# Gated embedding and down bias on four row strips, the loop's bias product on eight 32x32 tiles

## The chip, the cores and the metric

One Trainium2 chip, one of its cores, one launch. The metric is the device time of the whole program in microseconds (us). TensorE is PE here, VectorE DVE, ScalarE ACT, GpSimd POOL, and SP the engine that issues most transfers.

## The reference, cut to what matters

The program runs two blocks on 512 tokens of width 1024, in fp32: a block of four mixers with a mixture of experts and a gated embedding, and then a second block of two layers. The change touches the experts' biases and the gated embedding:

```python
hg, hl = jnp.split(xblk @ w_gu[e] + b_gu[e], 2, axis=-1)     # every block of rows, of one expert e
...
y = sum over the 4 chosen experts of gate * (hidden @ w_down[e] + b_down[e])
ffn = alpha * x1 + y
x = layer_norm(ffn + sigmoid(ffn @ ple_gate) * (p @ ple_proj), ln2)   # the gated embedding
x = layer_norm([meta, x], ln_emb)                                      # the second block begins
```

The lines of `y` and below are written here in short for what the reference does in several functions.

## The kernel before

The program is written engine by engine, and each engine runs its instructions in the order in which they are written; semaphores tie the engines together. Three stretches matter.

**The loop over row blocks.** 32 iterations, each for 96 routed rows of one expert. PE multiplies with the gate and up weights (line 1350, 96 matmuls of 512 columns, four at a time on four 32-column strips of the array), then fetches the expert's bias row (`bias_rows`, line 1338), and then multiplies with the down weights (line 1432, 96 matmuls of 256 columns). `bias_rows` multiplies a one-hot [32 x 32] with the table of biases `b_all`, which lies as four quarters on four strips of 32 partitions; quarter j goes to PSUM partitions 32j to 32j+31 of bank 6. ACT copies the bank to `b_gu` (line 2279). Once ahead of the loop the same product and copy run for the first block. A profile shows each fp32 matmul as two records, one for each of its two passes over the array. SP loads the expert's six pieces of 2 MB (line 1893) as PE frees their slots.

**down_bias.** Behind the loop PE turns the gates of the four tiles of 128 tokens (`transpose`, shown as line 908) into rows 0 to 31 of one bank, DVE copies them to `gates_t` (line 3045), and PE multiplies each tile's gates with `b_down` in eight matmuls of depth 32, tile by tile (line 1330). All use partitions 0 to 31. DVE adds each result to alpha times `x1` into `ffn` (line 3050). Then DVE adds the four chosen experts' rows of each tile (line 3121); they are read back from memory by SP in one 2 MB load for each tile (line 1929). The load of tile 3 is issued when tile 0 is added, since it takes its place.

**gated_embedding.** PE makes 8 embedding products (`embed`, line 1453; a tile's half of 512 columns each) in `v_ring`, a ring of PSUM banks 0 to 2 that DVE frees, and 8 gate products (line 1468) in `a_ring`, banks 3 to 5, which ACT frees. Three embeddings go ahead of the gates and the others between them, with a claim of their bank each. ACT turns each gate product into a sigmoid (line 2295) and after a tile's two halves computes the two square roots of that tile's norms (`rows_root`, line 2046), for each of which it waits for DVE. DVE multiplies sigmoid and embedding (line 3136), adds to `ffn` (line 3137) and norms the tile twice. The norm of the 16 meta rows, the second block's first rows, stands behind tile 0's rows of line 3121. `layers()` follows; PE enters it when both rings are empty.

Of the kernel before, what the change touches and what calls it, by code (L numbers as in the profile page):

```python
# [20 lines left out]
P = 128  # L21
# [8 lines left out]
E = 32  # L30
# [436 lines left out]
def build(nc, io):  # L467
    with ExitStack() as ctx:
# [146 lines left out]
        gates_t = take(SEQ)  # L615
# [37 lines left out]
        h_t = y_t  # L653
# [246 lines left out]
        def _(pe):  # L900
# [369 lines left out]
            def mix_out():  # L1270
# [25 lines left out]
                for half in range(2):  # L1296
                    w = ws[half]
                    for t in range(TT):
# [7 lines left out]
                        if half == 1 and t >= 2:  # L1306
                            if t == 2:
                                pe.wait_ge(sem("router_landed"), 16 * 4)
                                pe.wait_ge(v_ring.drained, len(MIX_BANKS))
                            router(t - 2, jobs[t - 2])  # L1310
# [9 lines left out]
            def down_bias():  # L1320
                pe.wait_ge(sem("gates_ready"), 1)
                bank = v_ring.bank(pe)
                for t in range(TT):
                    mm = transpose(bank[0:E, t * P:(t + 1) * P], gates[:, t, :])
                job = v_ring.ship(mm)
                pe.wait_ge(v_ring.drained, job)
                for t in range(TT):
                    for half in range(2):
                        bank = v_ring.bank(pe)
                        v_ring.ship(pe.matmul(bank, gates_t[0:E, t * P:(t + 1) * P], b_down[0:E, half * 512:(half + 1) * 512],  # L1330
                                              start=True, stop=True))
# [113 lines left out]
            def gated_embedding():  # L1445
# [3 lines left out]
                def embed(n):  # L1449
                    t, half = divmod(n, 2)  # L1450
                    bank = v_ring.bank(pe)
                    for k in range(2):
                        mm = pe.matmul(bank, p_t[:, k, t * P:(t + 1) * P], w_proj[:, k * D + half * 512:k * D + (half + 1) * 512],  # L1453
                                       start=(k == 0), stop=(k == 1))
                    v_ring.ship(mm)

                for n in range(3):
                    embed(n)
                w = []
                turned_job = transposed_tile(ffn, 0, sem("ffn_ready"))  # L1460
                for t in range(TT):
                    pe.wait_ge(a_ring.drained, turned_job)
                    for half in range(2):
# [6 lines left out]
                        if 3 <= 2 * t + half + 2 < 2 * TT:  # L1470
                            embed(2 * t + half + 2)
# [355 lines left out]
            pe.wait_ge(v_ring.drained, v_ring.sent)  # L1827
# [3 lines left out]
        def _(sp):  # L1831
# [46 lines left out]
            sp.dma_start(b_down[0:E, :], io["b_down"]).then_inc(sem("router_landed"), 16)  # L1878
# [132 lines left out]
        def _(act):  # L2011
# [248 lines left out]
            def experts():  # L2260
# [6 lines left out]
                A.did(act.copy(b_gu, psum[:, BIAS_BANK, :]), bias_ready)  # L2267
# [1443 lines left out]
```

## Time and profile before

| | us |
|---|---|
| median of 3 runs | 3166.81 (3165.43 to 3167.59) |
| the profiled execution, its time | 3164.56 |
| its span, first to last instruction | 3162.7 |
| PE busy in the span | 3049.8 (96%) |
| the loop's line 1350 / 1432 / 1338 on the chain that ended last | 21% / 11% / 1% of the span |
| mean granted TensorE clock | 0.975 of full speed |

The span is what the profile's rows divide; the time of an execution is 1.9 us more. A row "20.60 PE psum L1350 x192" of the chain says that 192 records of line 1350 followed one another for 20.60 us with nothing else on the chain between them.

### The profile page before, as it was taken

How to read it: one execution, taken by the hardware profiler on the slowest of the kernel's cores; microseconds unless marked ns; L12 is line 12 of the kernel's file. 1: busy time of each engine (PE TensorE's matmuls, PEld its weight loads, DVE VectorE, ACT ScalarE, POOL GpSimd, SP SyncE). 2: the span in 40 equal slices, each digit the busy share in tenths (PEclk: the TensorE clock that was granted, in tenths of full speed). 3: DMA queues.
4: the chain of work that ended last, by engine and by line, in shares of the span. 5: the costliest groups of instructions: out<-in, count | busy, mean ns of one | idle time of the engine just before them, and what ended most of it. 6: DMA issues, size and time to landing. Idle time of an engine off the chain costs nothing.

```text
span 3162.7 us, 53140 instructions
## 1 busy us (share of the span) xinstructions
PE 3049.8 (96%) x22625; PEld 1725.8 (55%) x22625; DVE 1218.2 (39%) x2417; ACT 559.4 (18%) x1138; POOL 225.7 (7%) x288
## 2 busy tenths in 40 slices
PE   9888979999999999999999999999999999999999
PEld 3355545434343434333345667674786658675865
DVE  1633365332322223232365452436325462435131
ACT  1332231111111111111122220140102310140000
POOL 0000000221212121212100000000000000000000
PEclk9988979999999999999989999999999999999999
DMA  4100115999999999999863333343424253343442
GB/s 165 40 15 27 35 39 213 365 410 405 415 407 403 413 406 411 405 412 408 333 268 117 134 111 126 126 151 149 167 111 169 108 209 125 119 167 124 189 168 90
DMA packets 68398, 684.44 MB, mean 216 GB/s; under 512 B 12092, under 2 KB 14396, under 8 KB 25408
## 3 DMA queue, kind: packets, MB, share of 16 engines
q1 hardware_dynamic: 53488, 651.87, 51.9%
q0 software_dynamic: 11296, 26.05, 2.2%
q10 hardware_dynamic: 3504, 4.94, 0.5%
q8 instruction: 83, 1.36, 0.2%
q14 instruction: 27, 0.22, 0.0%
HBM read 675.00 MB, written 16.80 MB: 219 GB/s over the span
## 4 chain that ended last, share of the span: by engine, by line
PE 84%; DVE 4%; ACT 2%; issue 1%; DMA 0%; DVEq 0%; SPq 0%; ACTq 0%
PE psum L1350 21%; PE psum L1743 20%; PE psum L1720 11%; PE psum L1432 11%; PE psum L1677 3%; PE psum L1666 3%; PE psum L908 1%; PE psum L1468 1%; PE psum L1302 1%; PE psum L926 1%; PE psum L1784 1%; PE psum L1338 1%; PE psum L1524 1%; PE psum L1570 1%; PE psum L1453 1%; PE psum L1598 1%
## 5 line engine op out<-in xcount | busy, mean ns | idle before, releaser
L1350 PE MATMUL psum<-weight_ring,arena 128*32 128x512 f32 x6192 | 670.4, 592 | 0.0
L1743 PE MATMUL psum<-arena,weight_ring 128*128 128x256 f32 (+1 forms) x2816 | 636.0, 384 | 2.8 <-ACT arena L2394 2.8
L1743 PEld LDWEIGHTS psum<-arena,weight_ring 128*128 128x128 f32 x2816 | 528.3, 189 | 100.3 <-issue 12.9
L1350 PEld LDWEIGHTS psum<-weight_ring,arena 128*32 128x32 f32 x6192 | 201.5, 110 | 449.1 <-issue 434.1
L1432 PE MATMUL psum<-weight_ring,arena 128*32 128x256 f32 x6144 | 338.2, 380 | 0.0
L1432 PEld LDWEIGHTS psum<-weight_ring,arena 128*32 128x32 f32 x6144 | 196.9, 110 | 152.7 <-issue 26.8
L1720 PE MATMUL psum<-weight_ring 128*128 128x512 f32 x468 | 204.1, 593 | 4.9 <-DMA weight_ring<-down 3.6
L1720 PE MATMUL psum<-weight_ring,arena 128*128 128x512 f32 x470 | 206.1, 597 | 0.7 <-ACT arena L2394 0.7
L3460 DVE TENSOR_TENSOR weight_ring<-weight_ring,psum 128x256 f32<-128x256 f32 (+1 forms) x88 | 37.4, 425 | 430.4 <-PE psum L1743 428.3
L3105 DVE STREAM_TRANSPOSE arena<-arena 128x384 f32<-128x384 f32 x32 | 18.5, 579 | 457.5 <-PE psum L1350 457.5
L3360 DVE TENSOR_TENSOR weight_ring<-weight_ring 128x1024 f32<-128x1024 f32 (+1 forms) x140 | 157.2, 1172 | 9.3 <-PE psum L1720 9.0
L1720 PEld LDWEIGHTS psum<-weight_ring 128*128 128x128 f32 x468 | 88.5, 190 | 116.0 <-issue 108.8
L1720 PEld LDWEIGHTS psum<-weight_ring,arena 128*128 128x128 f32 x470 | 89.5, 191 | 112.8 <-issue 111.1
L3081 DVE TENSOR_TENSOR arena<-psum,arena 128x512 f32<-128x512 f32 x96 | 65.1, 678 | 210.2 <-PE psum L1350 210.2
L924 PE MATMUL psum<-arena,weight_ring 128*128 128x512 f32 x288 | 133.6, 614 | 10.9 <-DMA weight_ring<-weights 6.6
L2454 ACT ACTIVATE weight_ring<-psum 128x256 f32<-128x256 f32 (+1 forms) x88 | 34.0, 387 | 584.0 <-PE psum L1743 583.8
L2277 ACT ACTIVATE arena<-arena 128x256 f32<-128x256 f32 x96 | 40.1, 417 | 468.8 <-DVE arena L3083 468.8
L1677 PE MATMUL psum<-arena,weight_ring 128*128 128x272 f32 (+1 forms) x512 | 116.8, 386 | 0.0
L1677 PEld LDWEIGHTS psum<-arena,weight_ring 128*128 128x128 f32 x512 | 96.1, 189 | 19.9 <-issue 2.8
L1965 POOL DMA_INDIRECT arena<-token_rows,arena x99 | 101.1, 1021 | 80.1 <-DVE arena L3073 31.9
L1989 POOL DMA_INDIRECT y_tokens<-arena x96 | 97.0, 1011 | 49.7 <-POOL arena L1985 28.3
L924 PEld LDWEIGHTS psum<-arena,weight_ring 128*128 128x128 f32 x288 | 54.2, 195 | 76.6 <-issue 67.0
(468 smaller groups left out, 2850.5 us busy)
## 6 DMA issues: line engine op xcount, KB each, us to landing
weight_ring<-exp_gu SPq DMA_DIRECT2D x129, 2048.0 KB, 10.5
weight_ring<-weights SPq DMA_DIRECT2D x80, 2048.0 KB, 7.8
weight_ring<-exp_down SPq DMA_DIRECT2D x64, 2048.0 KB, 9.9
weight_ring<-down SPq DMA_DIRECT2D x48, 1024.0 KB, 6.3
weight_ring<-y_tokens SPq DMA_DIRECT2D x4, 2048.0 KB, 16.8
weight_ring<-ple_gate SPq DMA_DIRECT2D x2, 2048.0 KB, 12.8
weight_ring<-forget_rows ACTq DMA_DIRECT2D x12, 264.0 KB, 10.1
arena<-ln_mid POOLq DMA_DIRECT2D x3, 1024.0 KB, 5.5
```

The source lines that it names most:

```text
L924: mm = pe.matmul(bank, w[:, k, a:a + P], x_t[:, k, :], start=(k == 0), stop=(k == KT - 1))
L1350: mm = pe.matmul(psum[j * GROUP:(j + 1) * GROUP, g, :], xg[:, k // 4, g, k % 4 * GROUP:(k % 4 + 1) * GROUP], w[:, kk, j * 512:(j + 1) * 51 ...
L1432: mm = pe.matmul(psum[j * GROUP:(j + 1) * GROUP, 3 + g, 0:256], hid_t[:, g, k * GROUP:(k + 1) * GROUP], w[:, kk, j * 256:(j + 1) * 256], s ...
L1666: mm = pe.matmul(bank[:, 0:width], h2_t[:, k, OFF[t]:OFF[t] + P], w[:, k, 0:width], start=first, stop=last)
L1677: mm = pe.matmul(bank[:, 0:b - a], w[:, k, c:c + P], h2_t[:, k, a:b], start=first, stop=last)
L1720: mm = pe.matmul(bank, left[stationary][:, q, :], right[part][f][half][:, n, :], start=(q == 0 and name not in ADDED_TO), stop=(q == pairs ...
L1743: mm = pe.matmul(bank[:, 0:b - a], w[:, k, col:col + P], h2_t[:, k, a:b], start=(k == 0), stop=(k == KT - 1))
L1965: pool.indirect_dma_start(rows_in[:, g, :], None, token_rows, bass.IndirectOffsetOnAxis(ap=index[:, g:g + 1], axis=0), bounds_check=SEQ * ...
L1989: pool.indirect_dma_start(y_tokens, bass.IndirectOffsetOnAxis(ap=now_y[:, g:g + 1], axis=0), y_out[:, g, :], None, bounds_check=SEQ * TOP ...
L2277: T.did(act.activation(sig[:, g, :], swi[:, g, 0:256], ACT.Sigmoid, scale=SWIGLU_ALPHA), swish_given)
L3081: T.did(dve.tensor_tensor(swi[:, g, :], psum[:, g, :], b_gu, ALU.add), gu_drained)
L3360: V.did(dve.tensor_tensor(b[out[0]][out[1]], b[one[0]][one[1]], b[other[0]][other[1]], op), right_ready)
```

## The change

It has three parts. (1) `bias_rows` makes eight matmuls of 256 columns, each on a 32x32 tile of its own: quarter j of the gate biases from strip j to bank 6, and quarter j of the up biases from strip j+1 (the table in memory is rolled by one for it) to bank 7; ACT's copy reads both banks. (2) `down_bias` turns the gates of tile t into PSUM partitions 32t to 32t+31 by a matmul with the identity, so that DVE's copy is [128 x 128]; `b_down` is loaded four times, to four strips; and the eight matmuls use strip t for tile t, first half of all tiles first. (3) All eight embedding products stand ahead of the gates, in `a_ring`; ACT copies them to `embedded`, which takes the place of `x1`; DVE's multiplication reads that. The meta rows' root and norm move ahead, and PE enters `layers()` when DVE has added the last gated half.

```diff
@@ down_bias, PE
-                    mm = transpose(bank[0:E, t * P:(t + 1) * P], gates[:, t, :])
+                    mm = pe.matmul(bank[t * E:(t + 1) * E, 0:P], gates[:, t, :], ident, start=True, stop=True, skip_group_check=True)
                 job = v_ring.ship(mm)
                 pe.wait_ge(v_ring.drained, job)
-                for t in range(TT):
-                    for half in range(2):
-                        bank = v_ring.bank(pe)
-                        v_ring.ship(pe.matmul(bank, gates_t[0:E, t * P:(t + 1) * P], b_down[0:E, half * 512:(half + 1) * 512],
-                                              start=True, stop=True))
+                mark["biased"] = {}
+                for half in range(2):
+                    for t in range(TT):
+                        bank, own = v_ring.bank(pe), slice(t * E, (t + 1) * E)
+                        mark["biased"][t, half] = v_ring.ship(pe.matmul(bank, gates_t[own, :], b_down[own, half * 512:(half + 1) * 512],
+                                                                        start=True, stop=True, skip_group_check=True))
@@ bias_rows, PE
-                        quarter = slice(j * GROUP, (j + 1) * GROUP)
-                        mm = pe.matmul(psum[quarter, BIAS_BANK, :], one_hot[quarter, :], b_all[quarter, :], start=True, stop=True,
-                                       skip_group_check=True)
+                        out = slice(j * GROUP, (j + 1) * GROUP)
+                        for part in range(2):
+                            held = slice((j + part) % 4 * GROUP, ((j + part) % 4 + 1) * GROUP)
+                            mm = pe.matmul(psum[out, BIAS_BANK + part, 0:256], one_hot[held, :], b_all[held, part * 256:(part + 1) * 256],
+                                           start=True, stop=True, skip_group_check=True)
@@ gated_embedding, PE
-                for n in range(3):
-                    embed(n)
+                for half in range(2):
+                    for t in range(TT):
+                        bank = a_ring.bank(pe)
+                        for k in range(2):
+                            mm = pe.matmul(bank, p_t[:, k, t * P:(t + 1) * P], w_proj[:, k * D + half * 512:k * D + (half + 1) * 512],
+                                           start=(k == 0), stop=(k == 1))
+                        a_ring.ship(mm)
...
-                        if 3 <= 2 * t + half + 2 < 2 * TT:
-                            embed(2 * t + half + 2)
...
-            pe.wait_ge(v_ring.drained, v_ring.sent)
+            pe.wait_ge(sem("gate_used"), 2 * TT)
@@ loads, SP
-            sp.dma_start(b_down[0:E, :], io["b_down"]).then_inc(sem("router_landed"), 16)
+            for t in range(TT):
+                sp.dma_start(b_down[t * E:(t + 1) * E, :], io["b_down"]).then_inc(sem("router_landed"), 16)
@@ the loop's copy, ACT (ahead of the loop likewise)
-                    T.did(act.copy(b_gu, psum[:, BIAS_BANK, :]), bias_ready)
+                    T.did(act.copy(b_gu.rearrange("p (b n) -> p b n", b=2), psum[:, BIAS_BANK:BIAS_BANK + 2, 0:256]), bias_ready)
@@ gated_embedding, ACT
+                rows_root(A, 0, META)
+                for half in range(2):
+                    for t in range(TT):
+                        bank = a_ring.take(act)
+                        act.wait_ge(v_ring.drained, mark["biased"][t, half])
+                        A.did(act.copy(embedded[:, t, half * 512:(half + 1) * 512], bank), a_ring.drained)
                 transposed_tile(h_t, 0)
-                rows_root(A, 0, META)
@@ DVE: the meta rows' norm, and the gating
+                dve.wait_ge(sem("ln_landed"), 48)
+                dve.wait_ge(sem("meta_landed"), 16)
+                norm_rows(V, h2[0:META, 0, :], 0, ln_emb, sem("layer_start"), META)
...
-                    if t == 0:
-                        dve.wait_ge(sem("ln_landed"), 48)
-                        dve.wait_ge(sem("meta_landed"), 16)
-                        norm_rows(V, h2[0:META, 0, :], 0, ln_emb, sem("layer_start"), META)
...
-                        bank = v_ring.take(dve)
-                        then(dve.tensor_tensor(ple_gate[:, n % TT, :], ple_gate[:, n % TT, :], bank, ALU.mult), v_ring.drained)
+                        then(dve.tensor_tensor(ple_gate[:, n % TT, :], ple_gate[:, n % TT, :], embedded[:, t, part], ALU.mult))
```

What PE has before, from the loop's `bias_rows` to the first gates (908 is the transpose, 1330 the down bias, 1453 the embedding, 1468 the gates, 1392 and 1439 the loop's end):

```order
L1338 MATMUL psum<-arena 32x512 x4
L1432 MATMUL psum<-weight_ring,arena 32x256 x96
L1392 REGISTER_ALU
L1392 COMPARE_AND_BRANCH
L1439 ISA
L908 MATMUL psum<-arena 32x128 x4
L1330 MATMUL psum<-arena 128x512 x8
L1453 MATMUL psum<-weight_ring,arena 128x512 x6
L908 MATMUL psum<-arena 128x128 x8
L1468 MATMUL psum<-weight_ring,arena 128x512 x8
```

And PE in the change, at the same place:

```order
L1341 MATMUL psum<-arena 32x256 x8
L1435 MATMUL psum<-weight_ring,arena 32x256 x96
L1395 REGISTER_ALU
L1395 COMPARE_AND_BRANCH
L1442 ISA
L1324 MATMUL psum<-arena 32x128 x4
L1331 MATMUL psum<-arena 128x512 x8
L1456 MATMUL psum<-weight_ring,arena 128x512 x16
L908 MATMUL psum<-arena 128x128 x8
L1468 MATMUL psum<-weight_ring,arena 128x512 x8
```

The bias product has eight matmuls of half the width, and all sixteen embedding matmuls (two for each product) now stand ahead of tile 0's transposes.

What DVE has before from the copy of the gates to the end of the experts' rows (2933 to 2951 are the meta rows' norm):

```order
L3045 COPY arena<-psum 32x512
L3050 SCALAR_TENSOR_TENSOR arena<-arena,psum 128x512 x8
L3121 SCALAR_TENSOR_TENSOR arena<-weight_ring,arena 128x1024 x4
L2933 BN_STATS arena<-arena 16x6 x2
L2944 BN_AGGR arena<-arena 16x2
L2947 SCALAR_TENSOR_TENSOR arena<-arena,weight_ring 16x1024
L2949 RECIPROCAL arena<-arena 16x1
L2951 SCALAR_TENSOR_TENSOR arena<-arena,weight_ring 16x1024
L3121 SCALAR_TENSOR_TENSOR arena<-weight_ring,arena 128x1024 x12
```

And DVE in the change, at the same place:

```order
L3049 COPY arena<-psum 128x128
L3054 SCALAR_TENSOR_TENSOR arena<-arena,psum 128x512 x8
L2937 BN_STATS arena<-arena 16x6 x2
L2948 BN_AGGR arena<-arena 16x2
L2951 SCALAR_TENSOR_TENSOR arena<-arena,weight_ring 16x1024
L2953 RECIPROCAL arena<-arena 16x1
L2955 SCALAR_TENSOR_TENSOR arena<-arena,weight_ring 16x1024
L3128 SCALAR_TENSOR_TENSOR arena<-weight_ring,arena 128x1024 x16
```

The meta norm has moved from behind tile 0's rows to ahead of them.

What ACT has before at the start of the gated embedding (2253 copies transposes, 2046 is a root, 2295 a sigmoid):

```order
L2253 COPY arena<-psum 128x4x128 x2
L2046 ACT_TABLE_LOAD
L2046 ACTIVATE arena<-arena 16x1
L2295 ACT_TABLE_LOAD
L2295 ACTIVATE arena<-psum 128x512
L2253 COPY arena<-psum 128x4x128 x2
L2295 ACTIVATE arena<-psum 128x512
L2046 ACT_TABLE_LOAD
L2046 ACTIVATE arena<-arena 128x1 x2
L2295 ACT_TABLE_LOAD
L2295 ACTIVATE arena<-psum 128x512
```

And ACT in the change, at the same place:

```order
L2045 ACT_TABLE_LOAD
L2045 ACTIVATE arena<-arena 16x1
L2291 COPY arena<-psum 128x512 x8
L2252 COPY arena<-psum 128x4x128 x2
L2299 ACT_TABLE_LOAD
L2299 ACTIVATE arena<-psum 128x512
L2252 COPY arena<-psum 128x4x128 x2
L2299 ACTIVATE arena<-psum 128x512
L2045 ACT_TABLE_LOAD
L2045 ACTIVATE arena<-arena 128x1 x2
L2299 ACT_TABLE_LOAD
L2299 ACTIVATE arena<-psum 128x512
```

The meta root and eight copies of embeddings are new ahead of tile 0's transposes; the two roots of tile 0 still stand between its sigmoids and the first sigmoid of tile 1.

## Rows read from the trace of the kernel before

**Rows 1.** The page: shares of the chain that ended last.

```profile
PE 84%; DVE 4%; ACT 2%; issue 1%; DMA 0%; DVEq 0%; SPq 0%; ACTq 0%
```

**Rows 2.** The chain that ended last, loop: start us, us, what.

```profile
1545.65 10.50 PE psum L1432 x192
1556.15 20.60 PE psum L1350 x192
...
1576.75 0.99 PE psum L1338 x8
```

**Rows 3.** Line 1338: all its matmuls; its weight loads of one iteration.

```profile
L1338 PE MATMUL psum<-arena x264: 587/600/613, 560.2 to 1577.2; 32*32 32x512 f32 x132
...
646.09 0.15 PEld L1338 LDWEIGHTS psum<-arena 32*32 32x32 f32 x8 [0.84 <-issue]
```

**Rows 4.** Groups in 1741 to 1742.6: count, busy us, mean ns.

```profile
L1535 PE MATMUL psum<-arena,weight_ring 64*128 64x256 f32 x4 | 0.7, 428 | 0.0
```

**Rows 5.** Window: busy PE, PEld, DVE, ACT, POOL, clock, DMA share, GB/s; landings, line 1893.

```profile
1000.00:1032.10 32.10, 32.10 (x396) 12.53 (x392) 9.25 (x25) 4.24 (x8) 6.47 (x8) 1.00 1.00 407
...
DMA to landing us min/median/max: 9.0/10.6/11.5
```

**Rows 6.** The chain that ended last, behind the loop.

```profile
1588.74 0.63 PE psum L908 x4
...
1589.38 0.69 DVE arena L3045
...
1590.12 11.10 PE psum L1330 x16
1601.22 8.12 PE psum L1453 x12
```

**Rows 7.** Timeline of DVE: start us, us, line, form, [idle before].

```profile
1591.35 1.48 DVE L3050 SCALAR_TENSOR_TENSOR arena<-arena,psum 128x512 f32<-128x512 f32 x2 [1.28 <-PE psum L1330]
...
1602.35 5.25 DVE L3121 SCALAR_TENSOR_TENSOR arena<-weight_ring,arena 128x1024 f32<-128x1024 f32 x4 [0.40 <-DMA weight_ring<-y_tokens]
...
1613.92 15.81 DVE L3121 SCALAR_TENSOR_TENSOR arena<-weight_ring,arena 128x1024 f32<-128x1024 f32 x12
```

**Rows 8.** Line 1929, loads of the rows of tiles 1 and 3.

```profile
L1929 SPq DMA_DIRECT2D weight_ring<-y_tokens x1: 434/434/434, 1595.8 to 1595.8; - x1
...
DMA to landing us min/median/max: 17.7/17.7/17.7
...
L1929 SPq DMA_DIRECT2D weight_ring<-y_tokens x1: 359/359/359, 1607.6 to 1607.6; - x1
...
DMA to landing us min/median/max: 15.9/15.9/15.9
```

**Rows 9.** The chain that ended last, gates and what follows them.

```profile
1642.94 0.87 PE psum L908 x8
1643.81 6.87 PE psum L1468 x16
...
1684.21 0.61 ACT arena L2295
...
1685.79 0.64 PE psum L908 x4
```

**Rows 10.** Timeline of ACT and DVE in the gates.

```profile
1629.97 0.69 DVE L3136 TENSOR_TENSOR arena<-arena,psum 128x512 f32<-128x512 f32 x1 [0.24 <-DVE arena L3121]
...
1638.89 0.29 ACT L2046 ACTIVATE arena<-arena 128x1 f32<-128x1 f32 x1 [3.99 <-DVE arena L2944]
...
1660.49 0.60 ACT L2295 ACTIVATE arena<-psum 128x512 f32<-128x512 f32 x1
```

**Rows 11.** Windows (columns as in rows 5); waits of PE, 1588 to 1686.

```profile
1593.10:1606.80 13.70, 13.70 (x17) 5.19 (x16) 8.38 (x10) 0.00 (x0) 0.54 (x1) 0.50 0.82 328
...
1630.70:1634.10 3.40, 3.38 (x4) 1.50 (x5) 3.13 (x5) 0.00 (x0) 0.00 (x0) 0.50 0.94 308
...
PE psum L1453 <- DVE arena L3136: 3.5, 1, 3.5
```

More of the change, by code:

```diff
@@ L614, in build @@
         picked, first_at = take(TT * TOP).rearrange("p (t n) -> p t n", t=TT), take(TT)
-        gates_t = take(SEQ)
+        gates_t = take(P)
         top, top_i, gate4 = (take(TT * 8).rearrange("p (t e) -> p t e", t=TT) for _ in range(3))
@@ L651, in build @@
         given_rows = ring[:, 0:3 * PIECE].rearrange("p (b n d) -> p b n d", b=3, n=TOP)
-        h_t = y_t
+        h_t, embedded = y_t, x1
         p_t = arena[:, at_mix + 3 * D:at_mix + 3 * D + 2 * SEQ].rearrange("p (k s) -> p k s", k=2)
@@ L1307, in mix_out @@
                             if t == 2:
-                                pe.wait_ge(sem("router_landed"), 16 * 4)
+                                pe.wait_ge(sem("router_landed"), 16 * (3 + TT))
                                 pe.wait_ge(v_ring.drained, len(MIX_BANKS))
@@ L1447, in gated_embedding @@
                 pe.wait_ge(sem("token_rows_landed"), 16 * 3)
[L1449 to L1455, printed above, removed]
-                for n in range(3):
-                    embed(n)
+                for half in range(2):
[5 more added lines that the diff above has]
+                        a_ring.ship(mm)
                 w = []
@@ L2266, in experts @@
                 act.wait_ge(bias_filled, 1)
-                A.did(act.copy(b_gu, psum[:, BIAS_BANK, :]), bias_ready)
+                A.did(act.copy(b_gu.rearrange("p (b n) -> p b n", b=2), psum[:, BIAS_BANK:BIAS_BANK + 2, 0:256]), bias_ready)
                 act.wait_ge(sem("routed"), 1)
@@ L2966, in mix_out @@
                         if half == 1 and t == 2:
-                            dve.wait_ge(sem("router_landed"), 16 * 4)
+                            dve.wait_ge(sem("router_landed"), 16 * (3 + TT))
                             choose(0)
@@ L3044, in down_bias @@
                 bank = v_ring.take(dve)
-                then(dve.tensor_copy(gates_t[0:E, :], bank[0:E, :]), v_ring.drained)
-                for t in range(TT):
-                    for half in range(2):
+                then(dve.tensor_copy(gates_t, bank[:, 0:P]), v_ring.drained)
+                for half in range(2):
+                    for t in range(TT):
                         part = slice(half * 512, (half + 1) * 512)
@@ L3644, in layout_block1 @@
     b_gu = np.asarray(a["exp_b_gu"])[0].reshape(E, 2, 4, 1, 256).transpose(0, 2, 3, 1, 4)
-    io["b_gu"] = np.ascontiguousarray(b_gu.reshape(E, 4, 512).transpose(1, 0, 2)).reshape(P, 512)
+    gate, up = b_gu.reshape(E, 4, 2, 256).transpose(2, 1, 0, 3)
+    io["b_gu"] = np.concatenate([gate, np.roll(up, 1, 0)], 2).reshape(P, 512)
     io["ple_gate"] = units(np.asarray(a["ple_gate_w"])[0])
```

## The prediction

> **What bounds the kernel now.** The page comes first. PE carries 84% of the chain that ended last [rows 1], so what PE does not do, or does not wait for, is what counts. The chain through the loop has only three kinds of pieces: 20.60 us of gate and up products, 0.99 us of the bias product and 10.50 us of down products [rows 2]. They add to 32.09 us, and the window over one iteration shows PE busy for all of it [rows 5]. Nobody makes PE wait in the loop, so a shorter bias product shortens each iteration, unless another engine or the DMA takes it back.
>
> Behind the loop the chain changes hands [rows 6]: turning the gates 0.63, DVE's copy 0.69, down bias 11.10, three embeddings 8.12. The clock explains part of it: from 1593.1 to 1606.8 PE was granted 0.50 of full speed, its lower level of 1.2 GHz, and again from 1630.7 to 1634.1, behind a wait of 3.5 us for DVE [rows 11]. DVE has the experts' rows meanwhile: tile 0 from 1602.35, tiles 1 to 3 from 1613.92 to 1629.7 [rows 7]. Gates are 6.87 us each and a tile's transposes 0.87 [rows 9].
>
> **Part 1, the bias product.** Full-speed cost of one pass: 10.50 / 192 x 4 = 0.219 us for 256 columns and 20.60 / 192 x 4 = 0.429 us for 512, four records at a time [rows 2]. The stage today is two passes of 512, 0.858, plus 0.13 for changing the array's tiling and starting: 0.99. That the four matmuls run at once is seen in line 1338's records: 600 ns each, eight of them in a stage of 0.99 us [rows 2, 3]. Its eight weight loads, some 103 ns each, begin and end within 0.15 us, so instructions start about 7 ns apart [rows 3].
>
> Eight tiles at once would take two passes of 256, 0.438, plus 0.13, plus 4 x 7 ns for four more tiles: 0.60 us, 0.39 less. What the loop does not show is two tiles in the same column strip, fed from different row strips. The nearest row is line 1535, two matmuls of 64 rows on all 128 columns into different banks: four records of 428 ns are done in 0.7 us of busy time, where 1.7 would be their sum, so row strips do share the columns [rows 4]. The reverse, four column strips with four different streams on the same rows, is line 1350 itself. I take 0.39. It comes 32 times in the loop and once ahead (264 records, 8 each, are 33 [rows 3]): **12.9 us**. The bounds are nothing, if a column strip serves one tile at a time (the same columns in total), and the loss below.
>
> The Trainium skill (TensorEngine Tiling (Array Packing), Gotcha 1: PSUM Pressure) speaks against this: different row tiles cannot access the same PSUM bank simultaneously, and here four row strips write to bank 6 and four to bank 7. The trace disagrees so far: today's four tiles are four row strips writing to bank 6, and they overlap. The Trainium skill (TensorE: Matmul & The Clock Gate, Wait — 56ns, not 53.3ns?) also puts start-to-start at no less than about 25 ns; sixteen records would then need 0.4 us to start, and my estimate from that figure is a saving of some 0.24 us an iteration, 8 us in all. The 7 ns between the loads is this trace's answer, though it is of loads.
>
> ACT's copy moves as many elements from two banks; it has no wait of PE behind it. What could take the gain back is the DMA. An iteration's share is 1.00 at 407 GB/s, so it has little to spare [rows 5]. Suppose it has nothing: then each iteration of 31.7 us leaves it 0.39 us further behind, 12 us at the end. A piece is asked for when its slot's last use ends and is used again one iteration less one piece later, 32.1 - 5.2 = 26.9 us; it lands after 10.6 (11.5 at most), so 15.4 us are in hand [rows 2, 5]. Even the full backlog would not reach PE, and SP does not wait for landings.
>
> The three more loads of `b_down`, 128 KB each, go ahead of the first expert pieces on SP. A 2 MB piece takes 32.1 / 6 = 5.3 us of DMA time at most, so they delay the pieces by about 1 us; the router and the listing of rows lie between and hide it, and I cost it at nothing.
>
> **Part 2, down bias.** In times of the old trace: PE is released at 1588.74. Four turns at once save about 0.2 of 0.63, and DVE's copy of 128 columns instead of 512 about 0.4 of 0.69 [rows 6]. The eight products then overlap by row strips, three at a time for three banks. DVE starts 1.23 us after PE today (1590.12 to 1591.35 [rows 6, 7]) and needs 0.74 each (two in 1.48 [rows 7]): from about 1590.8 to 1596.7, or to 1598 at the low clock, instead of 1602. But DVE's next work is not ready. Tile 0's rows land at 1602.3, where DVE already waits for them for 0.40 [rows 7]. The meta norm (1607.6 to 1613.9 today, 6.3 us, a part of it a wait for ACT's root) fits ahead. Tile 1's rows land at 1595.8 + 17.7 = 1613.5, and tile 3's, asked for when tile 0 is added, at 1607.6 + 15.9 = 1623.5 [rows 8]. DVE begins tile 1 at 1613.9 today, so the norm only filled a wait for the DMA: without it tile 1 begins at 1613.5, and three tiles of 5.25 end at 1629.3 instead of 1629.7. What looks like 11 us on DVE is worth **0.4**.
>
> **Part 3, embeddings first.** PE begins them at about 1595.5. Eight products of 4 records (4 x 0.429 = 1.72) are 13.7 us, plus 3 to 5 for the low clock: done at 1612 to 1614, and tile 0's gates begin at about 1614 (1611 at best). Gates and transposes alone would end at 1614 + 55.0 + 2.6 = 1672. They will not, since ACT becomes the tie to DVE: behind tile 0's two sigmoids it waits for two roots, and DVE cannot begin tile 0's gating before 1629.3. Today the gating begins at 1629.97 and the second root comes at 1638.89 [rows 10], so now at 1638.2; with its 0.3, the table load of 1.28 and a sigmoid of 0.60, bank for bank, PE gets the next bank at about 1640.6. `a_ring` has three banks; PE will have made tile 1's first gates and tile 2's transposes by 1636 and stand still for 4 to 6 us. Then half 1 of tile 1 and half 0 of tile 2, 13.7 us, and transposes 0.9 lead to 1655.2. The next bank needs the sigmoid of tile 2's first half, behind tile 1's two roots. Today that sigmoid starts 9.8 us after the gates that the one before its roots takes (1643.81 + 6.87 = 1650.7, to 1660.5 [rows 9, 10]); now those end at 1647.6, so the bank is free at 1658.0. Three gates of 6.87 end at 1678.6, against 1684.2 today, where ACT takes the last one [rows 9].
>
> Two subtractions. The first standstill is longer than the 3.5 us behind which the clock fell to its lower level for 3.4 us [rows 11]; the same again costs 1.7. And PE now enters `layers()` behind DVE's addition, 0.7 us later than behind the multiplication (0.69 [rows 10]). PE resumes at 1685.79 - 5.6 + 1.7 + 0.7 = 1682.6: **3.2 us** gained. The bounds are 1 (the clock down twice) and 5 (not down).
>
> **The sum.** 12.9 + 3.2 = 16.1 us, 0.51%. The profiled execution's 3164.56 becomes 3148.5; it lies 2.2 below the median of the runs, so I predict 3166.8 - 16.1 = **3150.7 us**. Below 0.2%, 6.3 us, a measurement of this kernel can hardly tell a change from none.
>
> **Rivals.**
> - Only four tiles at a time. The second four's first pass would run with the first four's second: three passes of 0.219 and 0.16, 0.82 us, saving 0.17 x 33 = 5.6. With 3.2 behind the loop: 3158. For it: no row has more than four matmuls at once. Against it: the four of today are limited by nothing in the trace but their tiles.
> - Nothing in the loop: column strips serve one tile at a time, or ACT's copy or the DMA takes it back. 3166.8 - 3.2 = 3163.6, no change that can be told. Against it are lines 1535 and 1350.
> - Slower. Bank 6 or 7 takes one row strip after another: the stage becomes 4 x 2 x 0.219 + 0.13 = 1.88, 0.89 more each time, +29 us, less 3.2: 3193. It decides as soon as the stage exceeds 0.99 + 3.2 / 33 = 1.09 us. Eight records of 600 ns in 0.99 us speak against it. The Trainium skill's rule on banks (TensorEngine Tiling (Array Packing), Gotcha 1: PSUM Pressure) is this rival.
> - More behind the loop: the rows land earlier, or ACT's waits fall otherwise, and PE's own 1672 binds: 7 us more, 3144.
>
> **How the numbers follow.** Eight at once 0.74; four at once 0.08; nothing in the loop 0.07; slower 0.06; more behind the loop 0.05. The first case's own range is 3148 to 3154 (the two bounds behind the loop, and 0.05 us on the stage). With four at once and part of the early side, 3147 to 3158.5 holds 8 in 10. Faster: 0.74 + 0.08 + 0.05, less a little for a median that falls badly, 0.86. Same: 0.08. Slower: 0.06.
>
> **What the changed profile would show.** The stage of `bias_rows` on the chain at 0.60 us, the iteration at 31.7, PE without idle time in it, pieces of line 1893 landing later and later by up to 12 us if the DMA is full and steadily if not. Behind the loop: DVE's eight additions back to back; DVE waiting for tile 1's rows until some 25 us behind the loop's end; PE standing still for 4 to 6 us in front of tile 1's second gates, and for 2 to 3 in front of tile 2's, with ACT's sigmoid as the releaser. The prediction is wrong if the stage stays at 0.85 or more, if a wait for an expert's piece appears in the loop, or if the standstills are missing.

## The result and the profile after

| | before | changed |
|---|---|---|
| median of the runs, us | 3166.88 (4 runs, 3165.43 to 3167.59) | 3146.85 (4 runs, 3145.92 to 3152.28) |
| the profiled execution | 3164.56 | 3145.92 |
| its span | 3162.7 | 3144.1 |
| ratio of the runs | | 0.9943, 95% interval 0.9931 to 0.9955 |

The changed kernel is faster, by 0.45% to 0.69%. The forecast was 3150.7, with 3147 to 3158.5 as the range: the median lies at its lower edge, 0.15 us outside, and 1.2 us below the 3148 to 3154 that were said for the case which came true. The same program was run again among the experiments, with a median of 3152.3, 0.31% to 0.59% below before. All ten of its runs together have a median of 3149.3, 17.2 us below the 3166.4 of before in that second comparison. The forecast gain was 16.1.

The page of the changed kernel, shares of the chain by engine:

```profile
PE 83%; DVE 4%; ACT 2%; DMA 1%; issue 1%; POOL 0%; SPq 0%; DVEq 0%; POOLq 0%; ACTq 0%
```

Its chain through the loop, which answers to [rows 2] (start us, us, what):

```profile
1541.69 20.60 PE psum L1353 x192
1562.29 0.59 PE psum L1341 x16
1562.88 10.54 PE psum L1435 x192
```

The stage of the bias product (line 1341 now) takes 0.59 us instead of 0.99. All its records, which answer to [rows 3]:

```profile
L1341 PE MATMUL psum<-arena x528: 374/386/400, 558.0 to 1562.5; 32*32 32x256 f32 x176
```

The window of one iteration, and the landings of the loop's loads (line 1892) between 600 and 1500 us, which answer to [rows 5]:

```profile
1000.00:1031.70 31.70, 31.70 (x408) 12.57 (x404) 9.19 (x25) 4.26 (x9) 6.47 (x8) 1.00 1.00 406
```

```profile
DMA to landing us min/median/max: 8.7/10.1/11.4
```

Sixteen records of 386 ns lie in a stage of 0.59 us, so all eight tiles work at once: the eight records of a pass start 7 ns apart, and the second pass starts 0.24 us behind the first. PE is still busy for all of the iteration, and the pieces land no later than before (a median of 10.1 us; the kernel before has 10.3 over the same 900 us, and 10.6 in the shorter stretch of [rows 5]).

The one product ahead of the loop gained nothing. From the timeline of PE:

```profile
558.04 0.66 PE L1341 MATMUL psum<-arena 32*32 32x256 f32 x16
559.12 20.81 PE L1353 MATMUL psum<-weight_ring,arena 128*32 128x512 f32 x192 [0.42 <-issue]
```

From its start to the first gate product are 1.08 us, where before they were 0.99: the product is shorter, but PE then stands idle for 0.42 us. All eleven profiles with eight products show this (1.08 to 1.18). So 32 products of the 33 were shortened.

The timeline of PE behind the loop (start us, us, line, form, idle time before and who ended it):

```profile
1573.87 0.43 PE L1324 MATMUL psum<-arena 128*32 128x128 f32 x8 [0.49 <-ACT arena L2282]
...
1576.68 4.57 PE L1331 MATMUL psum<-arena 32*128 32x512 f32 x10 [0.84 <-DVE arena L3054]
1581.18 16.15 PE L1456 MATMUL psum<-weight_ring,arena 128*128 128x512 f32 x32
...
1598.99 7.13 PE L1468 MATMUL psum<-weight_ring,arena 128*128 128x512 f32 x16 [0.78 <-ACT arena L2252]
...
1624.60 14.00 PE L1468 MATMUL psum<-weight_ring,arena 128*128 128x512 f32 x32 [2.85 <-ACT arena L2299]
...
1642.09 20.87 PE L1468 MATMUL psum<-weight_ring,arena 128*128 128x512 f32 x48 [2.61 <-ACT arena L2299]
1665.20 2.57 PE L908 MATMUL psum<-arena 128*128 128x128 f32 x24 [2.24 <-issue]
```

The turns, the down bias, eight embeddings without a break, the gates with two standstills for ACT's sigmoid, and the first matmul of `layers()` at 1665.20. DVE's timeline meanwhile, with the waits for tile 0's and tile 1's rows:

```profile
1582.11 1.27 DVE L2937 BATCH_NORM_STATS2 arena<-arena 16x6 f32<-16x512 f32 x2
...
1587.26 5.25 DVE L3128 SCALAR_TENSOR_TENSOR arena<-weight_ring,arena 128x1024 f32<-128x1024 f32 x4 [0.95 <-DMA weight_ring<-y_tokens]
1597.34 15.87 DVE L3128 SCALAR_TENSOR_TENSOR arena<-weight_ring,arena 128x1024 f32<-128x1024 f32 x12 [4.83 <-DMA weight_ring<-y_tokens]
1613.42 0.69 DVE L3138 TENSOR_TENSOR arena<-arena 128x512 f32<-128x512 f32 x1 [0.21 <-DVE arena L3128]
```

The clock over the same stretch (windows, columns as in [rows 5], the third number from the end is the granted clock), which answers to [rows 11]:

```profile
1578.70:1585.60 6.90, 6.90 (x11) 2.67 (x11) 5.88 (x10) 0.88 (x2) 0.07 (x1) 0.51 0.67 250
1585.60:1670.80 85.20, 74.74 (x252) 36.01 (x254) 62.16 (x77) 27.33 (x43) 0.00 (x0) 1.00 0.50 202
```

It was at half speed (1.2 GHz) for 6.9 us only, and through both standstills at full speed (2.4 GHz). In the profile of before the half-speed stretches behind the loop add up to 17.1 us [rows 11].

**Where the time went, by landmarks.** The loop's last copy by ACT ends at 1573.83 now and at 1588.69 before; the layers' first matmul stands at 1665.20 and 1685.79 [rows 9]. So the 18.6 us of the span are made of four parts:
- 2.5 ahead of the loop's first down product (580.5 and 582.9), of which the two bias products that stand there account for 0.3;
- 12.4 from it to the last copy, 31 bias products of 0.40 less;
- 5.7 from the last copy to the layers (91.4 us instead of 97.1);
- 2.0 lost in the layers. The change does not touch them, and in the second profile of the changed kernel they take 1476.8 us, as before (1476.9), instead of 1478.9.

### The profile page after: what moved, and what is told of

Same layout as the page of the kernel before. It is cut to its first block, busy times and chain, and to the rows that moved or that the text cites. A ratio compares the mean times of both kernels' runs of the same rounds, so it can differ in the third digit from the quotient of the medians.

```text
span 3144.1 us, 53691 instructions
## 1 busy us (share of the span) xinstructions
PE 3033.1 (96%) x22893; PEld 1725.7 (55%) x22893; DVE 1216.0 (39%) x2417; ACT 564.3 (18%) x1146; POOL 225.8 (7%) x288
## 4 chain that ended last, share of the span: by engine, by line
PE 83%; DVE 4%; ACT 2%; DMA 1%; issue 1%; POOL 0%; SPq 0%; DVEq 0%; POOLq 0%; ACTq 0%
PE psum L1353 21%; PE psum L1741 20%; PE psum L1718 11%; PE psum L1435 11%; PE psum L1675 3%; PE psum L1664 3%; PE psum L908 1%; PE psum L926 1%; PE psum L1302 1%; PE psum L1782 1%; PE psum L1522 1%; PE psum L1468 1%; PE psum L1568 1%; PE psum L1341 1%; PE psum L1596 1%
## 5 line engine op out<-in xcount | busy, mean ns | idle before, releaser
L1741 PEld LDWEIGHTS psum<-arena,weight_ring 128*128 128x128 f32 x2816 | 529.3, 190 | 100.7 <-issue 12.9
L1718 PEld LDWEIGHTS psum<-weight_ring 128*128 128x128 f32 x468 | 89.1, 191 | 115.3 <-issue 109.2
L924 PE MATMUL psum<-arena,weight_ring 128*128 128x512 f32 x288 | 135.8, 623 | 10.1 <-DMA weight_ring<-weights 5.9
L1988 POOL DMA_INDIRECT y_tokens<-arena x96 | 97.1, 1011 | 49.7 <-POOL arena L1984 28.3
## 6 DMA issues: line engine op xcount, KB each, us to landing
weight_ring<-exp_gu SPq DMA_DIRECT2D x129, 2048.0 KB, 10.3
```

What stands on the lines that cost most here:

```text
L924: mm = pe.matmul(bank, w[:, k, a:a + P], x_t[:, k, :], start=(k == 0), stop=(k == KT - 1))
L1718: mm = pe.matmul(bank, left[stationary][:, q, :], right[part][f][half][:, n, :], start=(q == 0 and name not in ADDED_TO), stop=(q == pairs ...
L1741: mm = pe.matmul(bank[:, 0:b - a], w[:, k, col:col + P], h2_t[:, k, a:b], start=(k == 0), stop=(k == KT - 1))
L1988: pool.indirect_dma_start(y_tokens, bass.IndirectOffsetOnAxis(ap=now_y[:, g:g + 1], axis=0), y_out[:, g, :], None, bounds_check=SEQ * TOP ...
```

## The experiments

Twelve kernels. "Behind" is the time from the loop's last copy on ACT to the layers' first matmul, from the two timelines of the profiled execution; before it is 97.1, changed 91.4. "Layers" is the time from the same copy to a later point, PE's first matmul of line 1718 (1720 before, 1722 or 1723 in some others), the first long stretch of products in the layers; before it is 105.3, changed 101.2. It is needed because the clock fell right behind the first landmark in some profiles. Each of these times comes from one profile. Medians of before beside them were 3166.46 (`loop_only`, `same_tile`, `narrow`, `tiny`), 3166.62 (`strips_only`, `norm_back`, `roots_late`, `mixed_late`) and 3166.44 (the others).

| kernel | median us (runs) | ratio to before, 95% | iteration | behind | layers |
|---|---|---|---|---|---|
| loop_only | 3154.71 (4) | 0.9940 to 0.9974 | 31.69 | 98.3 | 107.9 |
| same_tile | 3160.69 (10) | 0.9973 to 0.9993 | 32.12 | 93.2 | 101.8 |
| narrow | 3144.70 (4) | 0.9913 to 0.9949 | 31.48 | 92.6 | 100.7 |
| tiny | 3132.80 (4) | 0.9884 to 0.9917 | 31.30 | 92.6 | 100.8 |
| strips_only | 3163.41 (11) | 0.9982 to 1.0000 | 32.09 | 96.5 | 104.7 |
| norm_back | 3153.72 (5) | 0.9947 to 0.9974 | 31.69 | 98.0 | 107.8 |
| roots_late | 3145.97 (5) | 0.9917 to 0.9944 | 31.69 | 87.7 | 98.6 |
| mixed_late | 3143.49 (5) | 0.9915 to 0.9942 | 31.69 | 88.9 | 99.2 |
| changed_again | 3152.30 (6) | 0.9941 to 0.9969 | 31.69 | 92.5 | 100.6 |
| strips_norm | 3164.39 (12) | 0.9985 to 1.0002 | 32.09 | 93.7 | 103.3 |
| roots_split | 3148.32 (5) | 0.9932 to 0.9959 | 31.69 | 90.4 | 100.2 |
| all_together | 3145.72 (6) | 0.9926 to 0.9952 | 31.69 | 88.4 | 97.1 |

### The loop's part alone: loop_only

Before, with the new `bias_rows`, ACT's two copies and the rolled table.

> The kernel before with the bias product on eight tiles alone; down bias, embeddings and the meta norm stay where they were. My theory: the stage takes 0.59 us instead of 0.99, 33 times, 13.2 us, and the rest of the gain lies behind the loop: 3166.9 - 13.2 = 3153.7 us, 3153 to 3155. Rival: most of the 20 us comes from behind the loop or from the clock, so that this version lands at 3157 or later; then the loop's period must be above 31.8 us. A second rival: part of the gain is only the place of half-clock stretches ahead of the loop, which would let this run fall 2 us to either side.

3154.71, 11.8 us below before. The iteration is that of the changed kernel, 31.69; the part behind the loop is not (98.3). That carries the first theory.

### What makes the stage short: same_tile, narrow, tiny

Edits of the changed kernel; `narrow` leaves half of the loop's bias out of the output and `tiny` nearly all of it:

```diff
@@ same_tile (and the table not rolled)
-                            held = slice((j + part) % 4 * GROUP, ((j + part) % 4 + 1) * GROUP)
+                            held = out
@@ narrow, here with n = 128; tiny with n = 16
-  pe.matmul(psum[out, BIAS_BANK + part, 0:256], one_hot[held, :], b_all[held, part * 256:(part + 1) * 256],
+  pe.matmul(psum[out, BIAS_BANK + part, 0:n], one_hot[held, :], b_all[held, part * 256:part * 256 + n],
```

> The changed kernel, but part 1 of each strip is fed from the same row strip as part 0: again eight products of 256 columns into banks 6 and 7, but on four tiles of the array, two products on each. My theory (eight distinct tiles at once are what saves): the stage goes back to four passes of 256, 0.99 to 1.03 us, 33 x 0.42 = 14 us slower than the changed kernel, 3160.8. Rival (shorter products or the second bank save, wherever they stand): it stays at 0.59 us and 3147.

> The changed kernel, but each of the eight tile products takes only 128 of its 256 columns; the other columns of the loop's bias are left out, so the output misses part of it. It splits the 0.59 us into columns and starts. My theory (two passes of 256 columns, 0.44, and 0.15 for the change of tiling and the starts): the stage is 0.15 + 0.22 = 0.37 us, 33 x 0.22 = 7.3 us less, 3139.6. Rival (sixteen records start about 25 ns apart, 0.40 us, and this is what the 0.59 consists of): the stage stays above 0.5 us, at most 3 us less, 3144 or more.

> The changed kernel, but each of the eight tile products takes only 16 of its 256 columns; nearly all of the loop's bias is left out of the output. My theory: the stage falls to 0.15 to 0.19 us, 33 x 0.41 = 13.5 us less, 3133.4, with the loop's period at 31.3 us and no wait for an expert's piece. Rival 1 (starts 25 ns apart): 0.5 us, 3144. Rival 2 (the DMA is at its limit, since its share is 1.00): waits for pieces appear in the loop and the time is above 3137.

One stage each from the chains of the three, in this order (the chain lists thirteen of the last one's sixteen records):

```profile
1519.67 1.02 PE psum L1341 x16
```

```profile
1526.87 0.38 PE psum L1341 x16
```

```profile
1518.38 0.21 PE psum L1341 x13
```

Eight products on four tiles take 1.02 us, about the 0.99 of four products of twice the width: it is the eight distinct tiles that halve the time, not narrower products or a second bank. With eight tiles 256, 128 and 16 columns give 0.59, 0.38 and 0.21: 0.21 for 128 columns in two passes (0.22 worked out from [rows 2]), and some 0.15 to 0.18 that no column explains. In all three, the records of a pass start 7 ns apart. The Trainium skill (TensorE: Matmul & The Clock Gate, Wait — 56ns, not 53.3ns?) puts start to start at no less than about 25 ns. By that figure sixteen records would need some 0.4 us, an estimate; `narrow` and `tiny` are below it, so in these traces the floor does not hold for small tiles side by side. `tiny` also answers for the DMA: at 31.30 us an iteration PE has no wait in the loop between 600 and 1500 us, though the DMA share is 1.01. By time, `same_tile` and `tiny` came out as forecast, and `narrow` 5 us above, with two of its four runs at 3139 to 3141 and two at 3148 to 3149. Its median alone would have spoken for its rival (3144 or more); its stage of 0.38 us does not, since the rival needed more than 0.5.

### The down bias alone: strips_only

Part 2 of the change on the kernel before, the meta norm left behind tile 0's rows.

> The kernel before with the down bias on four row strips alone: its turns, its copy, its eight products and b_down's three more loads. Loop's bias product, embeddings and meta norm stay as they were. My theory: DVE's additions end 4 to 5 us earlier, but DVE then waits for y_tokens, so 0 to 1 us in all by DVE's path; PE begins its embeddings earlier and may keep 1 us of it: 3166 to 3167, not to be told from before. Rival: the down bias is where the 5.7 us behind the loop come from, then 3161 to 3163.

Behind the loop 96.5 instead of 97.1, or 98.3 in `loop_only`, which has the same code there: 0.6 to 1.8 us. The median is 3.2 us lower, with an interval that ends at 1.0000. The landmarks speak for the first theory, about 1 us for the part alone; the median (3163.4) is nearer to the rival's 3161 to 3163 and does not decide.

### The place of the meta norm: norm_back and strips_norm

```diff
@@ norm_back, from changed, on DVE: the norm behind tile 0's rows; on ACT:
-                rows_root(A, 0, META)
                 for half in range(2):          # the eight copies of the embeddings
 ...
                 transposed_tile(h_t, 0)
+                rows_root(A, 0, META)
```

> The changed kernel with the meta norm put back behind tile 0's expert rows, on DVE and with its root on ACT behind tile 0's transposes. My theory: the norm (4.2 us) again fills DVE's wait of 4.8 us for tile 1's rows, so DVE's end of the rows moves by at most 0.5 us: 3146.9, within 0.5 us. Rival: the norm's early place is worth its 4.2 us: 3151.

A clear miss: 98.0 behind the loop, 6.6 us more than in the first profile of the changed kernel, and a median 4.4 us above that of the changed kernel's ten runs (whose slowest overlap with it, so that the landmarks and not the time carry this). From the timelines of ACT, DVE, DVE and PE in `norm_back`:

```profile
1599.86 0.29 ACT L2045 ACTIVATE arena<-arena 16x1 f32<-16x1 f32 x1
...
1600.18 0.15 DVE L2953 RECIPROCAL arena<-arena 16x1 f32<-16x1 f32 x1 [5.12 <-ACT arena L2045]
...
1601.57 15.81 DVE L3125 SCALAR_TENSOR_TENSOR arena<-weight_ring,arena 128x1024 f32<-128x1024 f32 x12
...
1628.77 16.05 PE L1468 MATMUL psum<-weight_ring,arena 128*128 128x512 f32 x32 [6.21 <-ACT arena L2299]
```

The window of its half-clock stretch:

```profile
1626.10:1632.90 6.80, 4.13 (x5) 1.86 (x6) 4.38 (x7) 3.15 (x5) 0.00 (x0) 0.50 1.03 441
```

ACT's root stands behind the copies of tile 0's transposes, these behind PE's transposes, and these now behind eight embeddings. So DVE waits 5.12 us for the root, begins tile 1's rows 28.1 us behind the loop's last copy instead of 23.5, and PE's first standstill grows to 6.21 us. This time the clock fell, 3.5 us into the standstill, for 6.8 us, of which PE was busy for 4.1, and two gates took 16.05 instead of 14.00. Rows and standstill explain 4.6 us, the clock 2.0.

> The kernel before with the down bias on four strips and the meta norm (and its root on ACT) ahead of the expert rows; the embeddings stay between the gates and the bias product stays on four tiles. My theory now: with the norm out of the way DVE ends the rows 39.4 us behind the loop's last copy instead of 41.05 (40.40 with the strips alone), and the layers begin 95 to 96 us behind it instead of 97.1: 1 to 2 us, 3164.5 to 3165.5. The 6.6 us that the norm's place was worth in the changed kernel are then there only because the embeddings ahead of the gates hold up ACT's root. Rival: the norm's place is worth 4 us or more by itself, layers at 93 us.

93.7 behind the loop, 2.8 us better than the strips alone: more than my theory, less than its rival. DVE's rows end 39.3 us behind the last copy, as expected, and the half-clock stretch at `strips_only`'s first standstill (3.4 us) is not there. What the embeddings' move adds is the rest, 93.7 to the 91.4 to 93.2 of the five profiles with the changed code there: 0.5 to 2.3 us. The median of `strips_norm` is 2.1 us below before, with an interval that takes in 1, and 1.0 us above that of `strips_only`: by time the norm's place shows nothing here, and the 2.8 us rest on one profile of each.

### The standstills: roots_late, roots_split

```diff
@@ ACT, roots_late (roots_split puts the first of the two roots ahead of the sigmoid)
                         if half == 0 and t + 1 < TT:
                             transposed_tile(h_t, t + 1)
-                    if t + 1 < TT:
-                        rows_root(A, t)
-                        rows_root(A, t)
+                        if half == 0 and t > 0:
+                            rows_root(A, t - 1)
+                            rows_root(A, t - 1)
```

> The changed kernel with ACT's two roots of tile t behind the first sigmoid and the transposes' copies of the next tile instead of ahead of them. My theory (the two standstills of PE, 2.85 and 2.61 us, are ACT's order and a ring of three banks): both vanish, PE is through the gates 5.5 us earlier, DVE's own chain (four multiplications and additions and two norms, 11.6 us a tile from 1613.4) ends at 1651 and does not bind: 3146.9 - 5.5 = 3141.4. Rival 1 (DVE binds, the roots come later and hold up its norms): 0 to 2 us, 3145 or more. Rival 2: slower by up to 2 us, as the third standstill moves to the transposes' copies.

Timelines of PE, DVE and PE in `roots_late`:

```profile
1627.16 13.98 PE L1468 MATMUL psum<-weight_ring,arena 128*128 128x512 f32 x32
...
1629.69 0.16 DVE L2953 RECIPROCAL arena<-arena 128x1 f32<-128x1 f32 x1 [4.75 <-ACT arena L2045]
...
1667.04 1.30 PE L908 MATMUL psum<-arena 128*128 128x128 f32 x5 [4.35 <-issue]
```

Both standstills are gone and the gates end 5.8 us sooner behind the loop (83.3 instead of 89.1). So the tie is shown: ACT's order of roots and sigmoids. (That the ring has three banks belongs to the account; the number was not varied.) But the roots come late, DVE waits 4.75, 2.88 and 1.91 us for them, and PE then stands 4.35 us in front of the layers instead of 2.24: 3.7 of the 5.8 remain, between theory and rival 1. In that standstill the clock fell as well, and nearly all of the stretch lies behind the landmark:

```profile
1666.20:1676.40 10.20, 8.60 (x100) 7.33 (x104) 8.46 (x14) 4.48 (x10) 0.00 (x0) 0.50 0.32 134
```

At the later landmark 98.6 stands against 100.6 to 101.8, so 2.0 to 3.2 us remain.

> The changed kernel with ACT's first root of tile t ahead of the next tile's first sigmoid, and the second one behind it and the transposes' copies. In the version with both roots late PE ended its gates 5.8 us earlier, but DVE waited 4.75, 2.88 and 1.91 us for roots and held the layers up by 4.35 us. My theory: DVE's wait for the first root goes, at most 1.4 us a tile stays for the second; PE has its early end and the layers begin 85.5 us behind the loop's last copy instead of 91.4 (87.65 with both late), 6 us: 3141. Rival: the third pair of table loads delays the sigmoids and PE stands still again, 88 us or more.

90.4 behind the loop and 100.2 at the later landmark: the rival. ACT reaches the first root only when the sigmoid ahead of it is done, and each split costs one more pair of table loads; PE stands still 1.42 us twice, and DVE waits 2.13 us three times.

### The embeddings in the gaps: mixed_late, all_together

In both PE's order behind the turns is three biases, an embedding, two, an embedding, two, an embedding, one, five embeddings.

> The same late roots, and PE makes its embeddings between the products of the down bias, while it would wait for DVE to free banks: three biases, an embedding, two, an embedding, and so on. My theory: the stretch from the loop's end to the first gates (25.1 us in the changed kernel) becomes 1.1 + 8 x 1.72 + some 3 = 18 to 20 us, so gates begin at 1592 to 1594, but tile 1's rows are there only at 1602.6 and hold PE up again; DVE's chain ends at 1651 and PE's at 1653: 3 us more than the late roots alone, 3138. Rival: the embeddings delay the biases, DVE's additions and its request for tile 3's rows, and nothing is gained over late roots alone.

Behind the loop 88.9, against 87.7 with the late roots alone: the rival, for a reason I had not seen. From the timelines of PE and ACT:

```profile
1587.96 10.55 PE L1338 MATMUL psum<-weight_ring,arena 128*128 128x512 f32 x20 [3.22 <-ACT arena L2296]
...
1587.14 0.29 ACT L2050 ACTIVATE arena<-arena 16x1 f32<-16x1 f32 x1 [12.04 <-DVE arena L2953]
```

ACT waited 12 us for the meta norm's variance with three finished embeddings in its ring.

> The split roots, the embeddings between the products of the down bias, and the meta norm behind tile 0's rows on DVE, with its root on ACT behind the eight copies of the embeddings and ahead of the transposes' copies (in the version with mixed embeddings the root ahead of the copies kept ACT idle for 12 us and PE waiting for 3.2). My theory: tile 0's rows end 18.7 us behind the loop's last copy, gates begin at 20.5 instead of 25.2, PE then waits about 1.5 us for tile 1's rows; the layers begin 82 to 84 us behind the copy: 3138. Rival: DVE's chain, which begins at 39.6 with tile 3's rows however early PE is, and is 3 x 13 + 3 us long, binds: 85 us, 3140 to 3141.

88.4: both the theory (82 to 84) and its rival (85) were too low. The root's new place removes ACT's wait, but PE finds tile 0's transposes not copied. It stands still for 2.36 us, and 1 us into the gates the clock is at half speed for 3.4 us:

```profile
1598.54 8.83 PE L1473 MATMUL psum<-weight_ring,arena 128*128 128x512 f32 x16 [2.36 <-ACT arena L2257]
```

DVE's chain begins here as late as in the others, 39.9 us behind the loop, with the last tile's rows. None of these four versions can be told from the changed kernel's ten runs (3142.74 to 3154.72) by its time. At the later landmark `all_together` is the best of all (97.1, 3.6 to 4.7 us ahead of the five profiles with the changed code), which "behind" hides: there it is 88.4 against the 87.7 of `roots_late`.

### The same program again: changed_again

> The changed kernel once more, as it is, as the measure of what two executions of one program differ by. Two profiled programs with the same instructions ahead of the loop came to its first down product at 580.5 and 586.0 us. My theory: this is the clock's half-speed stretches in the mixers, and it moves the whole span by some 3 us to either side: median between 3144 and 3150, 51.1 us a pair of nothing else changed: loop's period 31.69, 91.4 us from the last copy of the loop to the layers' first matmul, to within 1 us. Rival: the part behind the loop varies as much as the part ahead of it.

(The "51.1 us a pair" in it is a slip and stands for nothing.) 3152.3 as a median, 2.3 above my range, while its profiled execution took only 3142.74. In the profiles the iteration is the same to 0.01 us, the part behind the loop is 92.5 instead of 91.4, the later landmark is at 100.6 instead of 101.2, and the part ahead of the loop is 578.3 instead of 580.5. Over all fourteen profiles the loop's first down product stands between 578.3 and 589.3, with no order by kernel: `roots_late`, with the same instructions up to there as the changed kernel, is at 586.0. The half-clock stretches lie elsewhere in each, and add up to 119 us ahead of the loop in `changed_again`, 130 in the changed kernel and 133 in `same_tile` (589.2); but `roots_late` also has 130. That they are the whole cause is not shown.

## Why the prediction was right

**The loop, 12.9 us: right.** The stage was put at 0.60 and measured 0.59. The sum counted it 33 times; the one ahead of the loop gave nothing, and 32 times 0.40 is 12.8. `same_tile` shows that eight tiles are the reason, `narrow` and `tiny` that the cost is columns in two passes and a fixed part near 0.16, as the sum had it (0.13 and 0.03). The rivals of four tiles, of no gain and of banks one row strip at a time fall with the same number. The last goes by the Trainium skill (TensorEngine Tiling (Array Packing), Gotcha 1: PSUM Pressure), which states that different row tiles cannot access the same bank at the same time. This trace disagrees: it has four row strips writing into each of two banks at once, to different partitions, in 0.59 us. Two row strips writing to the same partitions of one bank were not tried.

**The DMA: right that it could not bind; the supposed backlog did not even begin.** Landings had a median of 10.1 us (10.3 before over the same stretch) and of 10.0 in `tiny`, whose iterations are 0.8 us shorter than before. A share of 1.00 did not mean that nothing was left: `tiny` moves 419 GB/s where 407 were moved before.

**Behind the loop, 3.2 us: right mechanism, too small, and above the bound of 5.** Down bias and embeddings went as forecast: DVE's additions ran from 2.1 to 8.2 us behind the last copy (2.1 to 8.0 forecast) and tile 0's gates began at 25.2 (25.3). The five profiles with the changed code there (changed, again, and the three of the loop's experiments) give 91.4 to 93.2, mean 92.4; the two with the old code 97.1 and 98.3, mean 97.7: 5.3 us (5.6 at the later landmark). Two terms were off.
- "What looks like 11 us on DVE is worth 0.4": it was worth 1.7 (rows done 39.4 us behind the last copy instead of 41.05). The 0.4 rested on one landing, tile 1's rows 24.8 us behind the copy [rows 8]. In all thirteen other profiles they are there after 23.3 to 23.8 us, `loop_only` among them, whose DVE still begins tile 1 at 25.2, behind the norm. So the norm hid the wait for the rows in one profile only, the one that was read; what made them late in it is not shown.
- "The same again costs 1.7": the clock did not fall at the first standstill. That was 2.85 us, not 4 to 6, because ACT's second root came 1.0 earlier behind the last copy than forecast (48.5, not 49.5; the rows again) and PE came 0.6 later (47.9, not 47.3). In `norm_back`, at 6.21 us, it fell. But the length of a standstill does not settle it: in `same_tile` the clock stayed up at the first one (2.99 us) and fell 1.3 us behind the second (2.61 us):

```profile
1664.20 22.56 PE L1468 MATMUL psum<-weight_ring,arena 128*128 128x512 f32 x48 [2.61 <-ACT arena L2299]
...
1665.50:1668.90 3.40, 3.40 (x5) 1.35 (x4) 0.65 (x1) 0.00 (x0) 0.00 (x0) 0.50 0.00 0
```

The 2.5 us between the forecast of the layers' start (93.9 behind the last copy) and 91.4 are about 1.7 of clock and 1.0 of the earlier root.

One rival is left open. Between the last copy and the layers the clock is at half speed for 17.1 and 20.5 us in the two profiles with the old code, and for 6.8 to 10.2 us in the five with the new. In `norm_back` 4.1 busy us at half speed cost PE 2.05 us; at that rate, an estimate, up to 4.6 of the 5.3 us went by way of the clock. Whether that belongs to the new order or to how the stretches happened to lie, no run separates.

**The standstills: right** in place, order and tie, the first one shorter than said. The second was put at 2 to 3 us and measured 2.61; the entry into the layers behind DVE cost what was said (2.24 us from the gates' end, in which ACT's 0.61 and DVE's two of 0.7 lie).

**What the sum did not see.** The three parts behind the loop are not a sum. The norm's place was costed as one of DVE's orders; by one profile each it is worth 2.8 us with the embeddings in their old place and 4.8 to 6.6 behind eight embeddings, because its root stands in ACT's queue. Of the 5.3 us the strips bring about 1, the norm 3 and the embeddings 0.5 to 2, an estimate, since profiles of one code differ by 1.2 to 1.8 there.

**What was luck.** The time of a run contains several us that belong to no part: -2.2 ahead of the loop and +2.0 in the layers in the first comparison, which cancelled in the span. The gain of the medians, 20.0 us there and 17.2 over all ten runs, lies on both sides of what the stages add up to, 12.8 and 5.3.

## What to carry to other kernels

Small fp32 products in the middle of a PE-bound loop are worth spreading over all free tiles of the array: the cost goes by columns in a tile, and one iteration multiplies it. When a step is moved, follow what it needs on each in-order queue, not only on the engine where it runs: a 16-row root became worth some 5 us or more. And a wait that hides a step in one profile should be looked up in a second execution before the step is costed at nothing. Landmarks inside the profile show where 2 us went when medians of five runs do not; take one more landmark behind the stage too, since a fall of the clock right behind it can take part of the gain back.

## What the runs showed of the hardware

- Eight 32x32 tiles of the array run at once, two to a column strip from different row strips, writing to different banks: sixteen records of 386 ns in 0.59 us, and sixteen short ones in 0.21. Their records start 7 ns apart.
- The same instructions ahead of the loop took 578.3 to 586.0 us in seven executions; the loop that followed took the same time to 0.01 us.
- A standstill of PE of 2.85 us left the granted clock at full speed; in one of 6.21 us at the same place it fell to half for 6.8 us. But one of 2.61 us (`same_tile`) and one of 2.36 us (`all_together`) were also followed by 3.4 us at half speed.
